# One key copy, rotated parts projected alone, and a softmax step cut in two, in a two-block transformer kernel

## The reference, cut to what matters

```python
# block 1, latent attention
q = (_rms(h_q, q_norm_g) @ w_uq).reshape(B, S, 8, 64 + 32)        # q_nope, q_rot
kv = (_rms(h_kv, kv_norm_g) @ w_ukv).reshape(B, S, 8, 64 + 64)    # k_nope, v
q_rot, k_rot = _rope(q_rot, cos, sin), _rope(h_kr, cos, sin)      # rotates 32 columns
s = (einsum('bqhd,bkhd->bhqk', qn, k_nope) + einsum('bqhr,bkr->bhqk', qr, k_rot)) * 96 ** -0.5
o = einsum('bhqk,bkhd->bqhd', softmax(s), v)
# block 2, grouped-query attention: query heads 4g..4g+3 read key head g
q, k = rope(rmsnorm(q, q_gain)), rope(rmsnorm(k, k_gain))         # 16 and 4 heads of 64
k_all, v_all = concat([k_c, k]), concat([v_c, v])                 # 256 context + 512 tokens
o = einsum('bkgqs,bskd->bqkgd', softmax(q k_all * 64 ** -0.5), v_all)   # and the same for context queries
```

## Time and profile before

| | us |
|---|---|
| median of 3 runs | 3534.79 (3534.28 to 3535.42) |
| the profiled execution's own time | 3535.24 |
| its span | 3533.3 |
| PE busy, of the span | 3338.9 (94%) |
| DVE busy | 1614.1 (46%) |
| ACT busy | 1027.5 (29%) |
| POOL busy | 1096.9 (31%) |

### The profile page before, as it was taken

The page is one execution under the profiler, slowest core; times in us unless marked ns, Lnnn a source line. Parts: engine busy times, 40 slices in busy tenths (PEclk is TensorE's granted clock), DMA queues, the critical chain, the costliest instruction groups (busy, mean ns, idle before and its releaser), DMA issues.

```text
span 3533.3 us, 75481 instructions
## 1 busy us (share of the span) xinstructions
PE 3338.9 (94%) x32731; PEld 2475.5 (70%) x32731; DVE 1614.1 (46%) x2738; ACT 1027.5 (29%) x1687; POOL 1096.9 (31%) x718
## 2 busy tenths in 40 slices
PE   8987899989988999989999989999999999989998
PEld 3435678633337766778888865558888888868886
DVE  3245742421127888344433460126666666643333
ACT  3034232311124255341111131243333333232221
POOL 0053142123323101143322230025555555334441
PEclk9999899989989999999999999999999999999999
DMA  4311054389971100211111114430000000012221
GB/s 162 126 53 78 24 195 188 112 327 378 360 282 63 48 2 1 96 48 72 64 68 48 72 49 179 171 126 8 15 16 15 15 16 11 3 72 97 106 108 48
DMA packets 63383, 346.39 MB, mean 98 GB/s; under 512 B 17322, under 2 KB 17338, under 8 KB 26320
## 3 DMA queue, kind: packets, MB, share of 16 engines
q1 hardware_dynamic: 40608, 293.62, 21.5%
q0 software_dynamic: 18736, 36.94, 3.1%
q10 hardware_dynamic: 3712, 11.01, 0.8%
HBM read 379.77 MB, written 28.84 MB: 116 GB/s over the span
## 4 chain that ended last, share of the span: by engine, by line
PE 81%; DVE 6%; DMA 4%; ACT 4%; issue 3%; POOL 1%; ACTq 0%; DVEq 0%; POOLq 0%
PE psum L484 24%; PE psum L496 11%; PE psum L497 11%; PE psum L498 11%; PE psum L2551 4%; PE psum L3534 3%; ACT arena L907 2%; PE psum L2578 2%; DMA ring<-in_wall,arena 1%; PE psum L514 1%; PE psum L3517 1%; PE psum L3821 1%; DVE stat L964 1%; PE psum L510 1%; PE psum L511 1%
## 5 line engine op out<-in xcount | busy, mean ns | idle before, releaser
L484 PE MATMUL psum<-arena 64*64 64x64 f32 (+5 forms) x13456 | 633.7, 236 | 45.9 <-issue 14.3
L484 PEld LDWEIGHTS psum<-arena 64*64 64x64 f32 (+2 forms) x13456 | 525.3, 139 | 115.3 <-issue 79.3
L544 POOL TENSOR_TENSOR ring_low<-ring,slab_high 128x2048 fp32r<-128x2048 f32 x66 | 304.0, 4620 | 605.1 <-ACT slab_high L537 605.1
L496 PE MATMUL psum<-h_high,slab_high 128*128 128x512 f32 (+1 forms) x1008 | 357.4, 355 | 2.6 <-POOL ring_low L544 2.6
L497 PE MATMUL psum<-h_low,slab_high 128*128 128x512 f32 (+1 forms) x1008 | 357.2, 354 | 0.0
L498 PE MATMUL psum<-h_high,ring_low 128*128 128x512 f32 (+1 forms) x1008 | 357.0, 354 | 0.0
L484 PE MATMUL psum<-arena,ring 128*128 128x512 f32 (+3 forms) x880 | 335.9, 542 | 1.8 <-DVEq L1457 1.0
L484 PEld LDWEIGHTS psum<-arena,ring 128*128 128x128 f32 (+2 forms) x880 | 163.4, 187 | 170.8 <-issue 161.8
L1114 DVE TENSOR_TENSOR arena<-arena,psum 128x512 f32<-128x512 f32 x66 | 39.5, 599 | 470.6 <-PE psum L498 466.4
L496 PEld LDWEIGHTS psum<-h_high,slab_high 128*128 128x128 f32 x1008 | 191.0, 190 | 29.3 <-POOL ring_low L544 2.8
L497 PEld LDWEIGHTS psum<-h_low,slab_high 128*128 128x128 f32 x1008 | 191.0, 190 | 26.4
(11 more groups left out here) (543 smaller groups left out, 6168.7 us busy)
## 6 DMA issues: line engine op xcount, KB each, us to landing
ring<-in_wall SPq DMA_DIRECT2D x181, 1024.0 KB, 5.5
arena<-in_wall SPq DMA_DIRECT2D x96, 1024.0 KB, 11.6
spill<-arena ACTq DMA_DIRECT2D x8, 768.0 KB, 11.4
arena<-spill POOLq DMA_DIRECT2D x16, 384.0 KB, 3.6
filters<-arena POOLq DMA_DIRECT2D x2, 2048.0 KB, 6.6
arena<-filters POOLq DMA_DIRECT2D x2, 2048.0 KB, 15.9
arena<-moe_out POOLq DMA_DIRECT2D x8, 512.0 KB, 7.2
arena<-in_tabs POOLq DMA_DIRECT2D x2, 1536.0 KB, 12.1
```

What stands on the lines that cost most here:

```text
L484: last = L.eng.matmul(out, a, b, start=(i == 0), stop=(i == len(pairs) - 1))
L496: L.eng.matmul(out, a_hi, b_hi, start=(i == 0), stop=False)
L544: L.eng.tensor_tensor(m.low[:, n % SLOTS, :], m.ring[:, n % SLOTS, :], m.high_of(n).bitcast(F32), ALU.subtract).then_inc(m.sem("slab_split ...
```

## The change

- Slab `in_krs` is gone; `in_kv` carries the key's 32 rotated columns and their swapped copy side by side, and one product of 64 rows makes both, after `sine_tensor` instead of before it. DVE reads it with three instructions over 32 partitions, after the second `sine_vector`.
- `uqs` holds only the rotated columns; one product of 128 rows serves four heads. DVE's sine product and addition run over 32 partitions. The bank of four heads is released after the fourth.
- The plain keys of two heads come from one product of 128 rows; ACT copies each head from its half.
- Block 2 projects each key head once (`CHUNKS = KC + 2`, one `qkv_k` slab). Query columns and `wo0` rows are permuted on the host (`PAIRED`), so that the two halves of a chunk belong to different key heads.
- With halves side by side and more than 512 keys (`A.parts`, only `R.att`) the second head's exponential is two instructions with two sums and two bank releases. PE waits for the second banks only ahead of the second span of scores. DVE adds the two sums.
- The reciprocal is taken over two columns. Its spread over 128 columns is a copy of its own: on POOL in block 2 (`pair_attention_pool`, placed in POOL's order around the split of the first two `wo0` slabs), on DVE in block 1.
- Both halves of x count on one semaphore.

The diff, cut to its core:

```diff
-    plain(("in_q", 1), ("in_kv", 1), ("in_krs", 1), ("decay", 1), ...
+    plain(("in_q", 1), ("in_kv", 1), ("decay", 1), ...
-    plain(("qkv_q", 4), ("qkv_k", 2), ("qkv_v", 1), ("wo0", 4))
+    plain(("qkv_q", 4), ("qkv_k", 1), ("qkv_v", 1), ("wo0", 4))
...
+        self.read_out2 = self.m.bank_free[(b + 1) % 8], self.freed[(b + 1) % 8]
... pair_attention_tensor
-                for bank_free, count in L.bank_frees:
+                if A.parts:
+                    exped_last[i % 2] = L.read_out2
+                for bank_free, count in L.bank_frees[:1] if A.parts else L.bank_frees:
                     L.eng.wait_ge(bank_free, count)
             for lo, w in A.spans:
-                for half, (ps, full) in enumerate(banks):
+                for half, (ps, full, frees) in enumerate(banks):
+                    if A.parts and lo > 0:
+                        for bank_free, count in frees[1:]:
+                            L.eng.wait_ge(bank_free, count)
                     last = matmuls(L, ps[:, lo:lo + w], A.score(*steps[i], half, lo, w))
...
                 if t < 2:
                     L.eng.wait_ge(*exped[s + t])
+                elif A.parts:
+                    L.eng.wait_ge(*exped_last[(i - 1) % 2])
... pair_attention_scalar
+                if A.parts and half == 1:
+                    L.eng.activation(A.probs[:, s, :BANK], ps[:, :BANK], ACT.Exp, bias=m.stat[:, s:s + 1],
+                                     accum_out=m.stat[:, 4 + s:5 + s]).then_inc(L.bank_free, 1)
+                    L.eng.activation(A.probs[:, s, BANK:], ps[:, BANK:A.keys], ACT.Exp, bias=m.stat[:, s:s + 1],
+                                     accum_out=m.stat[:, 12 + i % 2:13 + i % 2]).then_inc(L.bank_free2, 1)
+                    continue
... pair_attention_vector
-            L.eng.reciprocal(A.share[:, (i - 1) % 2, :].rearrange("p (a b) -> p a b", a=2),
-                             bcast(m.stat[:, 4 + s:6 + s], HD)).then_inc(m.sem("shares_spread"), 1)
+            if A.parts:
+                read, rest = last
+                L.eng.wait_ge(*read)
+                L.eng.tensor_tensor(m.stat[:, 5 + s:6 + s], m.stat[:, 5 + s:6 + s], rest, ALU.add).then_inc(L.step, 1)
+                L.eng.wait_ge(L.step, L.next_step())
+            if A.pool_shares:
+                L.eng.reciprocal(m.stat[:, 8 + s:10 + s], m.stat[:, 4 + s:6 + s]).then_inc(m.sem("share_made"), 1)
+            else:
+                L.eng.reciprocal(m.stat[:, 8 + s:10 + s], m.stat[:, 4 + s:6 + s]).then_inc(L.step, 1)
+                L.eng.wait_ge(L.step, L.next_step())
+                L.eng.tensor_copy(A.share[:, (i - 1) % 2, :].rearrange("p (a b) -> p a b", a=2),
+                                  bcast(m.stat[:, 8 + s:10 + s], HD)).then_inc(m.sem("shares_spread"), 1)
...
+def pair_attention_pool(L, m, A):
+    for i in range(len(pair_steps(A))):
+        s = 2 * (i % 2)
+        L.eng.wait_ge(m.sem("share_made"), L.nth("share_made"))
+        L.eng.tensor_copy(A.share[:, i % 2, :].rearrange("p (a b) -> p a b", a=2),
+                          bcast(m.stat[:, 8 + s:10 + s], HD)).then_inc(m.sem("shares_spread"), 1)
... mix_in_tensor
-    ps = L.next_bank()
...
-    matmuls(L, ps[0:QK], [(w[:, KC * P + k * QK:KC * P + (k + 1) * QK], h(k)) for k in range(KC)]).then_inc(L.bank_full, 1)
-    L.last_read()
     L.eng.wait_ge(m.sem("sine"), L.nth("sine"))
     sine_tensor(L, m, m.vec("hw2", 0, 64, parts=64), B.h1)
-    w = L.next_slab("in_krs")
...
-    matmuls(L, ps[0:QK], [(w[:, k * QK:(k + 1) * QK], h(k)) for k in range(KC)]).then_inc(L.bank_full, 1)
+    at = [KC * P + k * 2 * ROT for k in range(KC)]
+    matmuls(L, ps[0:2 * ROT], [(w[:, at[k]:at[k] + 2 * ROT], h(k)) for k in range(KC)]).then_inc(L.bank_full, 1)
... latent_tensor
     for h in range(NH1):
-        for a in (w, ws):
+        ps = L.next_bank()
...
+        matmuls(L, ps[0:QK], [(w[:, k * NH1 * QK + h * QK:k * NH1 * QK + (h + 1) * QK], B.aqn[:, k, :]) ...
+        if h % 4 == 0:
+            ps = L.next_bank()
...
+            matmuls(L, ps, [(ws[:, at[k]:at[k] + P], B.aqn[:, k, :]) for k in range(2)]).then_inc(L.bank_full, 1)
...
-    for h in range(NH1):
+    for h in range(0, NH1, 2):
...
-        matmuls(L, ps[0:NOPE], [(w[:, h * NOPE:(h + 1) * NOPE], B.akvn[:, 0, :])]).then_inc(L.bank_full, 1)
+        matmuls(L, ps, [(w[:, h * NOPE:(h + 2) * NOPE], B.akvn[:, 0, :])]).then_inc(L.bank_full, 1)
...
-CHUNKS = KC + 4
+CHUNKS = KC + 2
... the POOL program
-            split_slabs(L, m, SLABS["qkv_q"][2:] + SLABS["qkv_k"] + SLABS["qkv_v"] + SLABS["wo0"])
+            split_slabs(L, m, SLABS["qkv_q"][2:] + SLABS["qkv_k"] + SLABS["qkv_v"])
+            pair_attention_pool(L, m, R.att)
+            split_slabs(L, m, SLABS["wo0"][:2])
+            pair_attention_pool(L, m, R.catt)
+            split_slabs(L, m, SLABS["wo0"][2:])
```

More of the change, by code:

```diff
@@ L812, in pair_attention_tensor @@
     steps = pair_steps(A)
-    n, turned, exped = len(steps), {}, {}
+    n, turned, exped, exped_last = len(steps), {}, {}, {}
     for i in range(n + 2):
@@ L944, in pair_attention_vector @@
     steps = pair_steps(A)
-    n, exps = len(steps), {}
+    n, exps, exps_last = len(steps), {}, {}
     for i in range(n + 2):
@@ L1430, in latent_scalar @@
     L.next_bank()
-    for h in range(NH1):
+    for _ in range(NH1 + 2):
         L.next_bank()
-        L.next_bank()
-    for h in range(NH1):
+    for h in range(0, NH1, 2):
         ps = L.next_bank()
@@ L1438, in latent_scalar @@
         L.eng.wait_ge(L.step, L.next_step())
-        L.eng.sem_inc(L.bank_free, 1)
-        L.eng.activation(B.k[NOPE:QK, h, :], B.kr[NOPE:QK], ACT.Copy).then_inc(L.step, 1)
-        L.eng.wait_ge(L.step, L.next_step())
+        L.eng.activation(B.k[0:NOPE, h + 1, :], ps[NOPE:2 * NOPE], ACT.Copy).then_inc(L.bank_free, 1)
+        L.eng.wait_ge(*L.read_out)
+        for one in (h, h + 1):
+            L.eng.activation(B.k[NOPE:QK, one, :], B.kr[NOPE:QK], ACT.Copy).then_inc(L.step, 1)
+            L.eng.wait_ge(L.step, L.next_step())
     for t in range(4):
@@ L1464, in latent_vector @@
         L.eng.sem_inc(L.bank_free, 1)
-        ps = L.next_bank()
-        L.eng.wait_ge(L.bank_full, L.fill)
-        L.eng.scalar_tensor_tensor(B.rot_a, ps[0:QK], QK ** -0.5, B.sin, ALU.mult, ALU.mult).then_inc(L.step, 1)
+        if h % 4 == 0:
+            swapped = L.next_bank()
+            swapped_free = L.bank_free
+            L.eng.wait_ge(L.bank_full, L.fill)
+        rot, turned = B.q[NOPE:QK, h, :], B.rot_a[NOPE:QK]
+        L.eng.scalar_tensor_tensor(turned, swapped[h % 4 * ROT:(h % 4 + 1) * ROT], QK ** -0.5, B.sin[NOPE:QK], ALU.mult,
+                                   ALU.mult).then_inc(L.step, 1)
         L.eng.wait_ge(L.step, L.next_step())
-        L.eng.sem_inc(L.bank_free, 1)
-        L.eng.tensor_tensor(B.q[:, h, :], B.q[:, h, :], B.rot_a, ALU.add).then_inc(L.step, 1)
+        if h % 4 == 3:
+            L.eng.sem_inc(swapped_free, 1)
+        L.eng.tensor_tensor(rot, rot, turned, ALU.add).then_inc(L.step, 1)
         L.eng.wait_ge(L.step, L.next_step())
-    for _ in range(NH1 + 4):
+    for _ in range(NH1 // 2 + 4):
         L.next_bank()
```

76 lines of the change are left out of this document (37 added, 39 removed).

## The result

The changed kernel takes 3484.2 us (median of 4 runs, 3481.2 to 3487.1), the kernel before, beside it, 3535.1 us (3534.3 to 3539.0): a ratio of 0.9856, 95% interval 0.9842 to 0.9870, faster by 50.9 us. Run again in another comparison it took 3482.7 us, ratio 0.9854 (0.9834 to 0.9874).

A forecast was written before the change was run, and what follows sets the result against it. PE held 81% of the chain of waits; the 768-key step was bound by a ring hardly longer than PE's own work. 6.9 + 10.3 + 20.3 + 6.8 + 0.8 - 1.6 = 43.5 us gave 3491.3 us, range 3486 to 3500.

The forecast's parts named there:

- Key projection and latent stage: First stages, block 1: sixteen key records fewer, minus 6.9 us; 24 query records fewer in the latent stage, minus 10.3 us.
- a price that I named (up to 1.7): Start of the 512-key attention: four more slow PE records at the low clock would cost 1.7 us; nothing was added.
- Query and key stage: Block 2: two chunks fewer save 21.0 us of PE, DVE's chain starts 0.65 us late; minus 20.3 us.
- 768-key steps: Long attention: splitting the exponential shortens the ring by 0.22 us to 4.81, over 31 releases minus 6.8 us.
- My upper bound of 9.0 us: 768-key steps: most that could be gained, 31 times PE's idle time of 0.29 us per step.
- PE fills the step: Rival, 768-key steps: the step comes to 4.74 us and the first share is early; 3487.5 us, chance 0.05.
- 256-key steps: Short attention: no step shorter; last spread reciprocal minus 0.8 us, first share late behind POOL's slab splits plus 1.6.
- The wait for POOL that I had named as the sign: 256-key stage: one PE wait of 1.6 to 1.8 us ahead of the first share transposition would show the forecast right.
- The prediction's price for POOL: Start of the 256-key stage: first share waits for POOL's slab splits and copy, plus 1.6 us, bounds 1.2 and 2.0.
- The prediction of a dear spread: Rival, 256-key steps: POOL's copy at 3 us binds the steps, 19 us lost; 3513 us, chance 0.06.
- The other edits: 512-key attention: zero, hidden behind PE; two slab loads and one semaphore wait fewer: zero.
- the two rivals of a dear spread: POOL's copy dear in block 2's attentions: short steps only, 3513 us, chance 0.06; or kernel slower, 3541 us, chance 0.03.

The follow-up runs named there:

- the one with one signal: Changed kernel with the second head's exponential whole again and PE's scores waiting for one signal per head, without ACT's second one; 3494.7 us, ratio 0.9884.

## Why the prediction was right or wrong

*Key projection and latent stage: right.* 17.2 us up to the end of the 512-key attention, 17.2 forecast. That it fits to the tenth is luck: this point scatters by 2.7 us between profiles, and small errors cancelled. The first stage gave 0.3 less, ACT's copies 0.67 more, and the attention's first records at the low clock cost 0.67 (6.04 against 5.37), a price that I named (up to 1.7) and set at nothing.

*Query and key stage: right in both terms.* 21.0 us of PE, less 0.65 of DVE: in the two profiles the attention starts 16.53 us after the last root where it was 15.87, which is 0.66. What the prediction had no term for is the clock in the value products, 1.56 us more in three of the ten profiles with both parts, one of them of the changed kernel itself.

*768-key steps: the step that failed.* "The ring shortens by 0.22 us to 4.81, just above PE's 4.74." The 0.22 is right (0.21). Three things were not:
- The release's second part. Before, what PE waited for was ACT's queue, not the exponential: the earlier trace rows say `<-ACTq L911`. That is a signal which ACT gives after waiting for itself. The parts drop it: 0.12 us. 29 steps gave 9.44 us where 0.22 each makes 6.4, so this term holds 3.1 of the 4.7 us that the stage was off.
- PE's own time. 5.03 - 0.29 took the bracket of one row for all of PE's slack. PE without a gap takes 4.70; the rows of a pipelined engine overlap (a row of 0.33 us is followed 0.28 later), so a gap between two rows understates the idle time. My upper bound of 9.0 us was too low for the same reason: 9.44 were gained in 29 steps.
- The start of the stage. Counting only the releases of steps in mid-stream I had two more times 0.22 for the first and the last; they gave 2.07 us, the other 1.6 of the error, and 1.6 is what the bank on which the count stood was worth. That a count of banks runs through the whole program, and that the removed products shift it, stands in the code; the prediction left it out.

The rival "PE fills the step" was the right case for the step (chance 0.05), but it too had 4.74 and no start.

*256-key steps: both terms right, their sum 0.45 us off.* Forecast -0.8 and +1.6, measured +0.35 together. The last step fell from 1.62 to 0.89 us, 0.73 less. The first share came 1.5 us later (6.18 against 4.66). The steps between gave another 0.4, which was no term: one more of them ran at 2.07 before the ring of 2.28 closed, and a stray of 2.43 is gone.

The wait for POOL that I had named as the sign isn't in the changed kernel's profile. There both engines are late: POOL copies the share at 1346.83, right behind its splits, so it is ready near 1347.1, and PE arrives at 1347.19 at the low clock. Two other kernels separate the two. In the one that starts on bank 2 and the one with one signal the granted clock is 1.00 from the stage's first scores to the first share, PE waits 1.45 and 1.46 us for POOL, and the share comes at +6.18 us. PE's timeline in the first:

```profile
1348.92 0.66 PE L872 MATMUL psum<-arena 128*64 128x128 f32 x8
1351.03 0.33 PE L875 MATMUL psum<-tabs,arena 128*128 128x128 f32 x1 [1.45 <-POOL arena L1036]
```

In the kernel with the long first reciprocals the share is ready early, the clock is low, and it comes at +6.16. So each alone costs 1.5 us, and both together no more. The prediction's price for POOL was right; that the clock can hide it was missing. The prediction of a dear spread counted thirteen steps of 2.2 us where the trace had 2.28 each, which changes nothing, as it did not come true.

Why the clock falls there isn't settled. In the ten profiles that have the key projection and block 1's parts together it falls 1 to 8 us after the stage's first scores and stays low for 3 to 14 us; in the kernel before and the three with one part alone it stays at 1.00 for the first 9 us (first share at 4.65 or 4.66 us). Ahead of it PE was idle for the same 0.82 and 0.92 us in the changed kernel and the one before. With the value products and the third pair of scores above, this is the third place where the same idle time was followed by either clock.

*The other edits:* nothing, as forecast. POOL's 48 copies of a share took 0.29 to 0.31 us each (0.4 taken, bounds 0.2 and 0.6), so the two rivals of a dear spread are out.

The sum with these terms: 17.2 + 20.3 + 11.5 - 0.35 = 48.7 us of the 50.7 between the two profiles; the other 2 us are scatter, 0.4 in the first interval of roots and 1.6 in the stretches outside the change. With the 768-key stage right the forecast would have been 3491.3 - 4.7 = 3486.6, still inside the range by 0.6 us, whose lower end was made of the same 4.74. That the time fell out by 1.8 us took the 0.45 of the 256-key stage and the 2 us of scatter as well.

## What to carry to other kernels

A wait on an engine's queue (`ACTq`) instead of on its instruction is a handshake that costs by itself, here 0.12 us in each of 29 steps: let each bank be released by the last instruction that reads it, and a whole instruction can be cut so that it does. When a ring and an engine's own work are within a few per cent, take the engine's own time from the spacing of its rows where it runs without a gap, not from the step less one bracket. Work removed anywhere ahead shifts the count of a rotating buffer, and with it which wait the next pipeline starts on.

## What was not expected of the hardware

A copy of 128x128 from SBUF to SBUF on DVE took 0.23 us alone and 3.31, 3.31 and 3.29 us in the three kernels in which it began 1.3 us into POOL's two-input slab split of 4.5 us, each time ending 0.07 to 0.09 us after the split. DVE's maxima and copies from PSUM, and its long reciprocal (0.95 us), ran beside the same split unhurt.

The changed kernel has this in its 512-key attention too, whose sixteen shares DVE spreads. The last five, with POOL idle, took 0.23 us each; those ahead of them, beside POOL's convolution, 0.23 to 0.95 us, and the longest ends at 271.30, again 0.08 us after POOL. It cost nothing there, since PE was busy for 64.63 of 64.66 us.

```profile
269.94 1.28 POOL L1525 TENSOR_TENSOR arena<-arena 128x512 f32<-128x512 f32 x1
```

```profile
270.35 0.95 DVE L999 COPY arena<-stat 128x128 f32<-128x128 f32 x1
274.22 0.23 DVE L999 COPY arena<-stat 128x128 f32<-128x128 f32 x1
```

The Trainium skill ("SBUF — State Buffer", the section on who interferes with whom) says that VectorE in a mode that uses two ports and GpSimd share a pair of ports under an exclusive lock, and that whoever comes second stands still for the whole instruction of the other. The three stalled copies agree with the standstill, up to the split's end; in which mode DVE made them no trace shows. The prediction had drawn on the rule only for instructions that read two tensors, and so held all of DVE's spreads for safe.
